# Where the copies of the key/value caches are issued: from GpSimd's queue to SyncE's, between its loads

## The reference

```python
for l in range(DEPTH):                      # DEPTH = 2
    mp, _    = mixer(xp, weights[l], past=None)
    ms, news = mixer(xs, weights[l], past=caches[l])
    xp, xs = post_norm(xp, mp), post_norm(xs, ms)
    xp, xs = post_norm(xp, moe_ffn(xp)), post_norm(xs, moe_ffn(xs))
# moe_ffn: router (d_model x 64), top 8 of 64 experts, one shared expert; each expert
#          silu(x @ w_gate) * (x @ w_up) @ w_down with 1024x256, 1024x256, 256x1024
# decoding: k_all = concat(cache_k, new_k); attention over its window
#          new cache = k_all[:, T:], v_all[:, T:]      with T = 4 new positions
```

## Time and profile before

| what | value |
|---|---|
| median of 3 runs | 1710.37 us (1709.98 to 1713.98) |
| profiled execution | 1715.04 us, its span 1713.2 us |
| mean granted clock of TensorE | 0.977 of full |
| TensorE, VectorE, ScalarE, POOL busy | 95, 28, 26, 16% |
| DMA engines: SyncE's and ScalarE's queue, POOL's | 72.6%, 9.9% of 16 engines' span |
| bytes moved | 481.67 MB and 58.41 MB |
| cache copies, DMAs | 32 from POOL |

### The profile page before, as it was taken

The page is one execution under the profiler, slowest core; times in us unless marked ns, Lnnn a source line. Parts: engine busy times, 40 slices in busy tenths (PEclk is TensorE's granted clock), DMA queues, the critical chain, the costliest instruction groups (busy, mean ns, idle before and its releaser), DMA issues. The chain is left out here.

```text
span 1713.2 us, 29473 instructions
## 1 busy us (share of the span) xinstructions
PE 1620.0 (95%) x11474; PEld 891.7 (52%) x11538; DVE 487.2 (28%) x1292; ACT 439.4 (26%) x850; POOL 270.0 (16%) x689
## 2 busy tenths in 40 slices
PE   7889999999999999999999679999999999999996
PEld 5564645454545444447577565564444444454543
DVE  2525522222222222222032333342222222222224
ACT  1243422222222222222022222422222222222223
POOL 0100421111111212100021300142121212121200
PEclk9889999999999999999999889999999999999998
DMA  9972399999899999939996976649999999999990
GB/s 299 293 249 90 150 386 371 361 364 368 358 368 357 368 357 368 358 146 373 331 385 228 343 270 237 266 167 395 362 368 358 367 357 371 354 376 350 375 353 29
DMA packets 105860, 540.82 MB, mean 316 GB/s; under 512 B 10773, under 2 KB 13589, under 8 KB 71636
## 3 DMA queue, kind: packets, MB, share of 16 engines
q1 hardware_dynamic: 102544, 481.67, 72.6%
q0 software_dynamic: 3200, 58.41, 9.9%
q10 hardware_dynamic: 68, 0.08, 0.0%
HBM read 535.69 MB, written 59.58 MB: 347 GB/s over the span
## 5 line engine op out<-in xcount | busy, mean ns | idle before, releaser
L1345 PE MATMUL ps<-ring,arena 128*64 128x512 f32 x2048 | 450.4, 592 | 1.6 <-ACT arena L1433 1.6
L1345 PEld LDWEIGHTS ps<-ring,arena 128*64 128x64 f32 x2048 | 148.0, 137 | 291.9 <-issue 290.2
L1365 PE MATMUL ps<-ring,arena 128*64 128x512 f32 x1024 | 233.8, 598 | 0.9 <-ACT arena L1438 0.9
L1320 PE MATMUL ps<-arena 128*128 128x128 bf16 (+1 forms) x3584 | 223.4, 219 | 1.9 <-POOL arena L1308 1.1
L1320 PEld LDWEIGHTS ps<-arena 128*128 128x128 bf16 (+1 forms) x3584 | 207.2, 98 | 18.6 <-issue 14.3
L1375 PE MATMUL ps<-arena 128*128 128x512 bf16 x704 | 162.4, 379 | 10.6 <-issue 9.9
L1433 ACT ACTIVATE arena<-ps 128x512 f32<-128x512 f32 x128 | 76.4, 597 | 350.3 <-PE ps L1320 350.3
L1308 POOL TENSOR_SCALAR arena<-arena 128x64 bf16<-128x64 f32 x384 | 160.3, 443 | 14.0 <-POOLq L1305 14.0
L1300 POOL COPY arena<-misc 128x64 f32 x64 | 15.3, 239 | 836.7 <-POOLq L1297 836.7
L1499 DVE TENSOR_TENSOR arena<-ps,arena 128x512 f32<-128x512 f32 x128 | 88.6, 692 | 167.2 <-ACT arena L1445 167.2
L1375 PEld LDWEIGHTS ps<-arena 128*128 128x128 bf16 x768 | 69.9, 98 | 126.5 <-issue 50.3
(11 more groups left out here) (320 smaller groups left out, 1342.9 us busy)
## 6 DMA issues: line engine op xcount, KB each, us to landing
ring<-in_w_exp_gate SPq DMA_DIRECT2D x128, 1024.0 KB, 7.8
ring<-in_w_exp_up SPq DMA_DIRECT2D x128, 1024.0 KB, 10.3
ring<-in_w_exp_down SPq DMA_DIRECT2D x128, 1024.0 KB, 6.9
out_dil_kv_sample<-in_cache_dil_kv POOLq DMA_DIRECT2D x8, 4080.0 KB, 33.8
ring<-in_w_in_odd SPq DMA_DIRECT2D x6, 3072.0 KB, 27.2
out_dil_kv_sample<-in_cache_dil_kv POOLq DMA_DIRECT2D x8, 2032.0 KB, 33.1
ring<-in_cache_dil_kv SPq DMA_DIRECT2D x4, 2048.0 KB, 34.4
ring<-in_cache_dil_kv SPq DMA_DIRECT2D x32, 256.0 KB, 9.6
```

Source lines behind the costliest of these rows:

```text
L1320: ins = pe.matmul(ps[:, TOK_A + hf, (c % 4) * P:(c % 4 + 1) * P], lhs, pm[0:m, q, k // 3, :], start=k == 0, stop=k == 6)
L1345: ins = pe.matmul(ps[64 * u:64 * u + CAP, WORK, :], MO["xg"][:, c, u * CAP:(u + 1) * CAP], w[:, c], start=c == 0, stop=c == NC - 1)
L1365: ins = pe.matmul(ps[64 * u:64 * u + CAP, TOK_A + hf, :], MO["hT"][:, j, 64 * u:64 * u + CAP], w[:, j, hf * BANK:(hf + 1) * BANK], start=j ...
```

## The change

All 32 copies move from POOL's list into SyncE's, through a new helper `shift(kind, rows)` whose DMAs have the same source, destination and shape. POOL's own helper and the two waits that stood in front of its dil3 copies go; its stores stay in their order. The places in SyncE's list:

- layer 0: dil3 of samples 0 to 3 behind the output weights; samples 4 and 5 behind the first expert's gate and up and in front of the wait for the mixer; samples 6 and 7 behind the second norm's parameters, in front of the fourth expert;
- layer 1: dil1 behind the cache loads of sample 0, swa and dil2 of samples 0 and 1 behind those of sample 1, dil2 of samples 2 and 3 behind those of sample 2, dil2 of samples 4 to 7 behind the second norm's parameters, in front of the fourth expert.

```diff
--- before.py
+++ after.py
@@ -2083,6 +2083,14 @@
                 for dst, src in parts:
                     sp.dma_start(dst, src).then_inc(s_ring[layer][slot_of(m)], 16)
 
+            def shift(kind, rows):
+
+                name, w = (("swa", P), ("dil1", WIN[0]), ("dil2", WIN[1]), ("dil3", WIN[2]))[kind]
+                dst, src = o[f"{name}_kv_sample"], a[f"cache_{name}_kv"]
+                for b in rows:
+                    sp.dma_start(dst[0, b, 0:w - TS].rearrange("k a h d -> k (a h d)"),
+                                 src[0, b, TS:w].rearrange("k a h d -> k (a h d)")).then_inc(s_copy, 16)
+
             def rows8(w):
                 return w.rearrange("(p c) n -> p c n", c=NC)
 
@@ -2180,15 +2188,18 @@
                 return parts
             load(0, 3, out_even(0))
             load(0, 4, out_even(1))
+            shift(3, range(4))
             load(0, 5, glu(slot_of(5), a["w_sh_gate"][0], a["w_sh_up"][0], a["w_sh_down"][0]))
             gain_bias(0, a["ln1_g"][0], a["ln1_b"][0])
             expert(0, 0, 0, True)
+            shift(3, (4, 5))
             sp.wait_ge(s_otc, 2)
             sp.wait_ge(s_mix[0], 8)
             router(0)
             expert(0, 0, 1, True)
             expert(0, 0, 2, True)
             gain_bias(1, a["ln2_g"][0], a["ln2_b"][0])
+            shift(3, (6, 7))
             expert(0, 0, 3, True)
             more = more_experts(0)
 
@@ -2214,6 +2225,13 @@
                 d2 = a["cache_dil2_kv"][0, b].rearrange("(k p) a h d -> p k (a h d)", p=P)
                 parts = [(ring[:, slot_of(6 + b), 0:4 * D].rearrange("p (k n) -> p k n", k=4), d2)]
                 load(1, 6 + b, parts + [(chunk_of(b, ck), rows_of(b, ck)) for ck in (5, 6)])
+                if b == 0:
+                    shift(1, range(NB))
+                elif b == 1:
+                    shift(0, range(NB))
+                    shift(2, (0, 1))
+                elif b == 2:
+                    shift(2, (2, 3))
             sp.wait_ge(s_ot, 2 + 8)
             sp.wait_ge(s_kst[1], 16 * 12)
             for b in range(4):
@@ -2248,6 +2266,7 @@
             expert(1, 0, 1, True)
             expert(1, 0, 2, True)
             gain_bias(3, a["ln2_g"][1], a["ln2_b"][1])
+            shift(2, range(4, NB))
             expert(1, 0, 3, True)
             more_experts(1)
             for t in range(3):
@@ -2263,16 +2282,6 @@
         def _(pool):
             pool.memset(EV["wg"], 0.0).then_inc(s_wg0, 1)
 
-            def shift(dst, src, w, rows=range(NB)):
-
-                for b in rows:
-                    pool.dma_start(dst[0, b, 0:w - TS].rearrange("k a h d -> k (a h d)"),
-                                   src[0, b, TS:w].rearrange("k a h d -> k (a h d)")).then_inc(s_copy, 16)
-            names = (("swa_kv_sample", "cache_swa_kv", P), ("dil1_kv_sample", "cache_dil1_kv", WIN[0]),
-                     ("dil2_kv_sample", "cache_dil2_kv", WIN[1]), ("dil3_kv_sample", "cache_dil3_kv", WIN[2]))
-
-            pool.wait_ge(s_ring[0][slot_of(4)], loaded(0, 4))
-            shift(o[names[3][0]], a[names[3][1]], names[3][2], range(4))
             n = 0
 
             def store(dst, src):
@@ -2292,8 +2301,6 @@
             assert 16 * n == OUT0
             moe_pairs_pool(pool, 0)
 
-            pool.wait_ge(s_ring[1][slot_of(3)], loaded(1, 3))
-            shift(o[names[3][0]], a[names[3][1]], names[3][2], range(4, NB))
             for i in range(4):
                 if i == 1:
                     item_copied(pool, at_item["v", 8, 0])
@@ -2303,10 +2310,6 @@
                         t0 = 1 if g == 0 else 0
                         store(o_p[0, 0, :, 1].rearrange("(t p) h d -> p t (h d)", p=P), OD["v"][:, t0:2, g, :])
                         store(o_s[0, :, WIN[g] - TS:WIN[g], 1].rearrange("b t h d -> b t (h d)"), OD["v"][0:NSA, 2, g, :])
-                    for dst, src, w in names[:2]:
-                        shift(o[dst], a[src], w)
-                if i == 2:
-                    shift(o[names[2][0]], a[names[2][1]], names[2][2])
                 if i == 3:
                     od_dec_prepare(pool)
                 for part in range(3):
```

## The result

| | before | after |
|---|---|---|
| median of 4 runs each, us | 1710.17 (1707.74 to 1713.98) | 1689.88 (1688.68 to 1691.59) |
| profiled span, us | 1713.2 | 1686.6 |
| mean granted clock | 0.977 | 0.989 |

After over before is 0.9876, 95% interval 0.9859 to 0.9892: 20.3 us less, and the forecast said 1690.

The account below looks back on a forecast made before the run. TensorE, busy 95% of the span, was taken to bound the kernel. The L1888 stretch gains 20.3 us, all else 0: 1715.04 - 20.3 = 1694.7 profiled, 1710.37 - 20.3 = 1690.1 at the median, said as 1690; range 1684 to 1702.

Parts of the forecast that it names:

- Both waits: TensorE's waits at L1888 for the cached keys of samples 2 and 3, 9.27 + 7.38 = 16.65 us, would go.
- Rival 3: At L1888 the two loads are late by themselves and the waits stay: 1708 to 1712 us, chance 0.04.
- The stretch: From TensorE's first L1888 to its first L1904: 30.04 us would become 9.7, gaining 20.3, of which 3.7 are clock.
- Rival 4: Low-clock stretches of the odd stage vanish or appear elsewhere: +-3 us around any case; far side's chance 0.03.
- K stores and SyncE's chain: SyncE's wait at L2218 for POOL's K stores, then for L1798: stores land in a few us, no cost.
- the fifth chunk: Fifth key chunk's loads in the odd stage: at worst held back 5 us by K stores, TensorE by some 4.
- Rival 1: The wait at L1888 only shrinks, SyncE's chain replacing it: gain 8 to 15 us, 1695 to 1702, chance 0.09.
- Parts 2, 3, 5: Copies behind w_out_even, copies before the router table, and POOL losing 32 issues of 0.5 us: 0 us each.
- Part 4: Each layer's last copies, in front of the fourth expert, hidden under shared-expert and routing work: 0 us.
- Rival 2: Copies before loads in SyncE's queue, as at the fourth expert, move at 170 GB/s: about 1721 us, chance 0.05.
- the room of 39.3 or 35.2 us: Time for copies before the fourth expert's gate and up become late, in layer 0 and layer 1 respectively.

Follow-up runs that it names:

- b_no_dil2: The kernel before the change without POOL's eight dil2 copies (16.6 MB), nothing else changed: 1688.71 us, ratio 0.9868 to the kernel before.
- a_dil2_pool: The changed kernel with only the eight dil2 copies given back to POOL at their old place: 1709.3 us, ratio 0.9983 to the kernel before.
- a_no_copies: The changed kernel with all 32 cache copies left out: 1689.52 us, ratio 0.9875 to the kernel before.
- a_l0_8: The changed kernel with all eight dil3 copies (33.4 MB) in front of layer 0's fourth expert, none earlier: 1753.36 us, ratio 1.0273 to the kernel before.
- a_l0_4: The changed kernel with four dil3 copies instead of two before layer 0's fourth expert, none behind its first: 1701.77 us, ratio 0.996 to the kernel before.
- a_dil2_front4: The changed kernel with all eight dil2 copies (16.6 MB) in front of layer 1's fourth expert: 1706.45 us, ratio 0.9991 to the kernel before.
- a_dil2_b2: The changed kernel with all eight dil2 copies behind sample 2's load in SyncE's queue: 1710.29 us, ratio 0.9998 to the kernel before.

## Why the prediction was right

- **Both waits go**: they did, by the mechanism forecast. b_no_dil2 and a_dil2_pool show from both sides that the copies of dil2 made them. Rival 3 is refuted.
- **The stretch**, 9.7 us forecast, is 8.98, and the gain in it 21.06 for 20.3. I let the clock come back at 972 on the old axis, which is 966.6 on the new one, 5.4 us earlier; it was back by 966.5. The forecast's parts fit: L1791 2.79 for 2.89, and the first sixteen transposes of L1888, run as twelve and four, 2.56 + 0.63 for 1.91 + 1.3. The gain minus the 16.65 us of waits leaves 4.4 us for clock, 3.7 forecast. Rival 4's further shifts did not come: the median moved by 20.3. That the median met 1690 to 0.1 us is luck: the stretch gave 0.8 us more than forecast, and the four runs before lie 6 us apart.
- **K stores and SyncE's chain**: forecast a few us, measured 2.2 at the median for the prompt's stores. SyncE's two waits are now these, where 28.8 and 14.7 stood in the earlier trace rows:

```profile
SPq L2236 <- DMA out_dil_kv_sample<-arena: 13.2, 1, 13.2
SPq L2238 <- PE ps L1798: 10.1, 1, 10.1
```

  They end at 962.9 and 973.1. The forecast had the second at 979 on the old axis, 973.6 on this one; for the first it said only a few us behind the stores, the last of which POOL issued at 961.2. No matmul waited for the fifth chunk. Rival 1 didn't happen.
- **Parts 2, 3, 5 at nothing**: borne out as a sum by a_no_copies (1689.52 against 1689.88). The router table is issued at 127.09, behind copies, and no matmul waits for it.
- **Part 4 at nothing**: the engines were done with the two copies of layer 0 by 202.5, 23 us before the second pair's L1345 at 225.41; with the four of layer 1 by 1113.9, where the next pair's L1345 begins at 1133.35 (the DMA view has the last copies landed some 4 us after that, still in time). Forecast were 211 and 1144 on the old time axis, which lies 5.4 and 26.5 us later there: 205.6 and 1117.5. So both were about 3 us earlier than forecast. The bounds that I gave, a cost only below 213 and 236 GB/s, were not touched: a_l0_8 has 339 GB/s in this queue.
- **Rival 2** had the right place and the wrong rate. Its place is real: 8.4 MB more than the change puts there cost 12 to 17 us of time (a_l0_4, a_dil2_front4), and 16.7 MB more than that another 49 us of wait. The prediction's own sum, all the bytes there at 334 GB/s less the room of 39.3 or 35.2 us, gives waits of 10.7, 60.8 and 14.6 us for a_l0_4, a_l0_8 and a_dil2_front4; measured were 11.46, 60.76 and 14.81. The Trainium skill's rule of ring order within a row ("DMA: Bandwidth & Descriptors", Queues, rings and completion order) agrees with a_dil2_b2 and a_l0_8, where no load passed a copy; it did not turn the change into a loss, because what stands in front of a load here moves under TensorE's work.

What I got wrong came after the prediction: four expectations took 356 to 367 GB/s for the copies, from stretches of about 23 us, and left the waits 5 to 8 us short each. The prediction's own 334, from a window of 46 us with nothing but copies, gives three of the four waits within 1 us, as just shown, and that of a_dil2_b2 within 2 (an estimate: 16.6 MB from 923 on, where sample 2's load had landed, and the 3.15 MB load behind them would be there at 981.4; it was 983).

## What to carry to other kernels

Bulk copies with no deadline belong where the compute engine is busy and the next load isn't yet due, in portions no larger than (bytes per us) x (us until that load is wanted, less its own transfer). Here 35 and 39 us at 334 GB/s hold 11.8 and 13.1 MB: 8.3 and 8.4 MB fitted, 16.6 and 16.7 did not. Which queue carries them made no difference once the moments were right; so ask of each copy which load is due while it moves. Take the rate for such a sum from a long window of copies, and read a wait of the bounding engine with the few us of low clock that follow it, since both go together.

## What the runs showed of the hardware

- A long backlog can stall the issuing engine itself. In a_l0_8 SyncE's first two issues behind the eight copies, at 204, took 0.3 and 0.5 us as usual; of the next four of their kind three took 12 to 28 us:

```profile
216.70 12.15 SPq L2118 DMA_DIRECT2D ring<-in_w_exp_gate  x1
228.95 22.01 SPq L2118 DMA_DIRECT2D ring<-in_w_exp_up  x1
251.16 0.58 SPq L2118 DMA_DIRECT2D ring<-in_w_exp_gate  x1
251.83 28.41 SPq L2118 DMA_DIRECT2D ring<-in_w_exp_up  x1
```

- Small stores in a queue of their own are slowed by large copies in the other one. In a_dil2_b2 POOL's K stores of the samples, twelve of 16 KB, landed 9.3 us after their issue at the median and 27.5 at most; in the changed kernel the median was 1.8:

```profile
DMA to landing us min/median/max: 1.7/9.3/27.5
```

- A wait costs more than its length, since low clock follows it. After one of 11.46 us (a_l0_4) the next 32 matmuls took 9.69 us instead of 7.04, and after one of 16.54 us (a_dil2_b2) 24 matmuls took 5.22 us instead of 2.79. The granted clock was 0.77 from 237 to 246 in the first case, and 0.50 (1.2 GHz) from 983.5 to 989 in the second. The addition doesn't grow with the wait: after 60.76 us (a_l0_8) the 32 matmuls took 8.96 us.
